# Output projection of a hybrid decoder layer: three fp32r products of split halves in place of one fp32 product, the second half of the projection token tile by token tile, and counters raised at another place

## The chip, the cores and the metric

One core of one Trainium2 chip runs the whole program. The metric is the device time of one execution in microseconds (us). Engines are named as the profile names them: PE is TensorE (PEld its weight loads), DVE VectorE, ACT ScalarE, POOL GpSimd, SP SyncE, which here only issues transfers; a q behind a name is that engine's sequencer.

## The reference, cut to what matters

```python
n = rms_norm(h, norm_mix_w)                     # h: 16 meta tokens + 512 tokens, width 1024
proj = n @ w_in                                 # conv_B | conv_C | conv_x | z | x,B,C of the SSD | dt
y_conv = grouped_rms_norm(c_b * causal_dwconv(c_c * c_x), 8 groups)
y_ssd  = grouped_rms_norm((ssd_chunked(...) + D * xs) * silu(z), 4 groups)
h = h + concat([y_conv, y_ssd]) @ w_out         # (512 x 2048) @ (2048 x 1024): the output projection
logits = rms_norm(h) @ router_w + router_b      # 32 experts, the best 4 of each token
h = h + sum of the 4 experts' clamped SwiGLU, gated
out = rms_norm(h)[16:]
```

All of it is float32. The 512 tokens give 2048 assignments to 32 experts, in blocks of up to 96 tokens per expert.

## The kernel before

Each engine has its own program in the order of the source, and they meet by semaphores: `wait_ge` stops an engine until a counter has reached a value, `then_inc` raises one when an instruction is done. An engine never passes a waiting instruction.

**Input projection and SSD.** A product of normed input and weights is made of fp32r parts. ACT copies a tile of 128x1024 weights to its rounded high part `w_hi` (L662), DVE subtracts that from the tile and gets the low part `w_lo` (L874, in the helper `split`), the input has `n_hi` and `n_lo` in the same way, and `mm3` (L1344) adds hi x hi, lo x hi and hi x lo into one PSUM bank. `w_hi` and `w_lo` have two buffers each. After 16 tiles of x, B and C come four chunks of 128 tokens (`chunk_step` on DVE, `turn_chunk` and `rest_of_chunk` on PE), which also make the conv heads and norm them (`head_norms`: two reciprocals at L964, two multiplies at L968). PE's products of a chunk (L1472) need from DVE the masked score (L996, fed by L984 to L989) and the C rows scaled by exp(a) (`e4`, L1004).

**The z tiles.** Eight tiles of 128x512 follow (k = 0 to 7, `pair(k, 0, SEQ)`, two pairs of banks in turn). ACT takes each by `Silu` (L767), DVE multiplies it onto y_ssd (L1100) and makes the low part of the weights two tiles on; `group_squares` and `group_norm` norm the four SSD groups on the way. Ahead of them DVE runs the last `head_norms` and four small router operations (L1083 to L1089).

**Output projection.** The 2048 rows of w_out are eight pieces r of 256 rows (1 MB each), the 512 tokens four tiles m. `out_proj(r, m)` (L1526, matmuls at L1530) is four fp32 matmuls of 128x128 by 128x512 that read y and w_out as they are; the profile has two records for each fp32 matmul and one for each fp32r matmul. The order is r = 0 to 3 for m = 0 to 2, then r = 4 to 7 for each of these m, and the last tile in eight steps (`last_tile`), for which w_out's pieces 0 and 1 are loaded again.

**Routing.** For each finished tile DVE adds the residual (`residual`, L1114), ACT squares it, DVE scales it and SP writes the normed rows to DRAM (`n2_scratch`, L419); PE transposes the tile (L1552), multiplies it by the router weights (`logit_parts`, `logits`), DVE chooses four experts (`choose`), PE ranks the tokens (`rank`), DVE places them (`place`, L1167 to L1177), and POOL scatters four columns of slots (L552). `pick_first` (L1595) gathers the first expert's tokens by a matmul; this part stands in small pieces between the steps of the last tile and behind it.

**Experts.** A block is `gate_up`, eight pieces q = 0 to 7 of 1 MB, and `down`, pieces 8 to 11, all at L1660. The weights lie in 12 slots of 1 MB: slots 0 to 5 in `ring`, 6 to 11 in `ring2`, which is free of the input's halves once the z tiles are through. The second expert's first two pieces go to `extra` (the regions reg_b and reg_x). SP refills a slot when PE has used it. The second expert's tokens come by POOL: four reads of the slot list (`list_rows`, L565), an add (L569), three indirect gathers (L573), then DVE turns them (L1256). `gate_up(0)` needs `x0T` (L1210), its pieces, and one count each of `xT_ready` and `gu_free`, which DVE raises by hand:

```python
            dve.sem_inc(gu_free, 1)
            dve.sem_inc(act_ready, 1)
            dve.wait_ge(bias_in, 16)
            up_bias = bias.rearrange("p (n k b) -> p n k b", k=2, b=FF_BLOCKS)[:, :, 1, :]
            v.tensor_scalar(up_bias, up_bias, 1.0, None, ALU.add).then_inc(bias_ready, 1)
            dve.sem_inc(xT_ready, 1)
```

## Time and profile before

| | us |
|---|---|
| median of 3 runs (1581.72 to 1583.81) | 1582.28 |
| the profiled execution, whole | 1586.74 |
| its span in the trace | 1585.1 |
| PE / DVE / ACT / POOL busy in the span | 1531.7 / 584.9 / 228.5 / 330.5 |

The span is one execution from its first to its last instruction, and all places below are microseconds from its start. A busy engine is in an instruction's record, and PE's records overlap, so that the pitch from start to start says what a matmul costs. A chain row is a piece of the chain of work that ended last; a number in square brackets behind a timeline row is the idle time ahead of it with what released it.

### The profile page before, as it was taken

The page shows a single profiled execution, that of the slowest core. Times are in us where ns is not written, and L with a number is a line of the kernel's source. Part 1 is how long each engine was busy: PE and PEld are TensorE (multiplying, and loading weights), DVE is VectorE, ACT ScalarE, POOL GpSimd, SP SyncE. Part 2 cuts the span into 40 slices and gives each one's busy share as a digit, 9 for nine tenths or more (in the row PEclk, how much of TensorE's full clock was granted, in tenths as well). Part 3 has the DMA queues.
Part 4 walks back from the last instruction along what each step waited for, and adds up shares of the span by engine and source line. Part 5 has one row for each costly group of instructions (what it writes and reads, how often), then busy time and mean ns, then how long its engine had stood idle before and what let it go on. Part 6 is the DMA issues. An engine that isn't in the chain of part 4 may idle for free.

```text
span 1585.1 us, 37739 instructions
## 1 busy us (share of the span) xinstructions
PE 1531.7 (97%) x15275; PEld 1000.5 (63%) x15275; DVE 584.9 (37%) x1221; ACT 228.5 (14%) x316; POOL 330.5 (21%) x512
## 2 busy tenths in 40 slices
PE   9999999999996999999999999999999999999996
PEld 7998899774442455655654665666556566666562
DVE  6777988862134321122211321122211321122225
ACT  4533443240021000000000000000000000000001
POOL 1000000000024232223322232223322232223320
PEclk9999999999998999999999999999999999999998
DMA  4232222334254999999999999999999999999936
GB/s 148 81 125 86 88 77 104 159 143 166 89 192 160 380 399 406 403 410 405 398 407 401 407 403 398 408 407 404 400 405 407 408 404 399 407 413 404 396 121 271
DMA packets 80788, 479.09 MB, mean 302 GB/s; under 512 B 17410, under 2 KB 18058, under 8 KB 26610
## 3 DMA queue, kind: packets, MB, share of 16 engines
q1 hardware_dynamic: 66354, 461.24, 73.0%
q0 software_dynamic: 14400, 17.37, 3.1%
q8 instruction: 24, 0.39, 0.1%
q14 instruction: 10, 0.08, 0.0%
HBM read 470.03 MB, written 17.01 MB: 307 GB/s over the span
## 4 chain that ended last, share of the span: by engine, by line
PE 92%; DVE 5%; issue 1%; DMA 1%; ACT 1%; POOLq 0%; SPq 0%; DVEq 0%; POOL 0%; ACTq 0%
PE bank L1660 65%; PE bank L1344 15%; PE bank L1530 7%; DMA moe_f<-in_b_gate_up 1%; PE bank L1363 1%; PE bank L1472 0%; PE bank L1475 0%; DVE w_lo L874 0%; PE bank L1473 0%; PE bank L1502 0%; DVE reg_tq L964 0%; DVE reg_tq L890 0%; PE bank L1487 0%; DVE reg_vcs L869 0%; PE bank L1721 0%
## 5 line engine op out<-in xcount | busy, mean ns | idle before, releaser
L1660 PE MATMUL bank<-ring,moe_f 128*32 128x512 f32 (+1 forms) x12240 | 1023.7, 486 | 21.9 <-DVEq L1264 10.1
L1660 PEld LDWEIGHTS bank<-ring,moe_f 128*32 128x32 f32 x12240 | 620.1, 110 | 425.0 <-issue 261.5
L1275 DVE STREAM_TRANSPOSE moe_f<-bank 128x768 f32<-128x768 f32 x32 | 31.4, 983 | 617.5 <-PE bank L1660 617.5
L1344 PE MATMUL bank<-n_hi,w_hi 128*128 128x258 f32 (+2 forms) x608 | 190.8, 314 | 7.2 <-DVE w_lo L874 4.9
L573 POOL DMA_INDIRECT moe_f<-n_scratch,idx_next x99 | 103.7, 1047 | 450.8 <-DVE moe_f L1256 415.3
L1344 PE MATMUL bank<-n_lo,w_hi 128*128 128x258 f32 (+2 forms) x608 | 187.1, 308 | 0.0
L1344 PE MATMUL bank<-n_hi,w_lo 128*128 128x258 f32 (+2 forms) x608 | 187.0, 308 | 0.0
L824 ACT ACTIVATE moe_f<-moe_f 128x768 f32<-128x768 f32 x32 | 27.1, 845 | 718.1 <-DVE moe_f L1279 718.1
L1344 PEld LDWEIGHTS bank<-n_hi,w_hi 128*128 128x128 f32 x608 | 115.0, 189 | 16.2 <-DVE w_lo L874 5.4
L580 POOL DMA_INDIRECT expert_rows<-moe_f,idx_now x96 | 98.5, 1026 | 104.5 <-ACT moe_f L830 82.9
L1344 PEld LDWEIGHTS bank<-n_lo,w_hi 128*128 128x128 f32 x608 | 115.0, 189 | 6.5 <-issue 1.2
L1344 PEld LDWEIGHTS bank<-n_hi,w_lo 128*128 128x128 f32 x608 | 114.9, 189 | 5.7
L1530 PE MATMUL bank<-ring,reg_vcs 128*128 128x512 f32 x256 | 111.9, 594 | 0.0
L1293 DVE TENSOR_TENSOR moe_f<-moe_f 128x768 f32<-128x768 f32 x32 | 30.7, 959 | 160.8 <-PE bank L1660 160.7
L1530 PEld LDWEIGHTS bank<-ring,reg_vcs 128*128 128x128 f32 x256 | 48.0, 190 | 57.8 <-issue 57.8
L565 POOL DMA_DIRECT2D idx_raw<-slot_table x140 | 72.7, 529 | 8.8 <-issue 8.4
L552 POOL DMA_INDIRECT slot_table<-val,pos_i x16 | 16.6, 1035 | 223.3 <-DVE pos_i L1177 219.6
L830 ACT COPY moe_f<-bank 128x768 f32<-128x768 f32 x32 | 25.6, 801 | 247.8 <-PE bank L1660 247.8
L874 DVE TENSOR_TENSOR w_lo<-ring,w_hi 128x1024 fp32r<-128x1024 f32 x48 | 58.5, 1220 | 5.7 <-ACT w_hi L662 5.7
L662 ACT CAST w_hi<-ring 128x1024 fp32r<-128x1024 f32 x48 | 50.6, 1054 | 50.2 <-PE bank L1344 49.9
L1285 DVE TENSOR_SCALAR moe_f<-moe_f 128x96 f32<-128x96 f32 x256 | 47.6, 262 | 0.0
L1279 DVE TENSOR_SCALAR moe_f<-moe_f 128x96 f32<-128x96 f32 x256 | 47.5, 261 | 0.0
(249 smaller groups left out, 806.5 us busy)
## 6 DMA issues: line engine op xcount, KB each, us to landing
ring<-in_moe SPq DMA_DIRECT2D x382, 1024.0 KB, 7.4
ring<-in_w_in SPq DMA_DIRECT2D x24, 1024.0 KB, 4.8
ring<-in_w_out SPq DMA_DIRECT2D x10, 1024.0 KB, 4.9
ring<-expert_rows SPq DMA_DIRECT2D x8, 1024.0 KB, 12.1
ring<-acs_scratch SPq DMA_DIRECT2D x4, 1024.0 KB, 7.6
idx_raw<-slot_table POOLq DMA_DIRECT2D x140, 0.8 KB
reg_vcs<-in_xT SPq DMA_DIRECT2D x4, 528.0 KB, 6.0
reg_x<-in_xrow SPq DMA_DIRECT2D x4, 512.0 KB, 6.1
```

Source lines behind the costliest of these rows:

```text
L565: pool.dma_start(idx_raw[l * LANE:(l + 1) * LANE, :], table_d[ds(base, BLOCK), :].rearrange("(r g) t -> r (g t)", g=GRANULES)).then_inc(id ...
L573: g.indirect_dma_start(out=xg[:, n, :], out_offset=None, in_=n2_parts, in_offset=bass.IndirectOffsetOnAxis(ap=idx_next[:, 2 * n:2 * n + 1] ...
L580: g.indirect_dma_start(out=yk_parts, in_=y_sb[:, n, :], in_offset=None, out_offset=bass.IndirectOffsetOnAxis(ap=idx_now[:, 2 * n + 1:2 * n ...
L662: a.copy(w_hi[:, n % 2, :], slot(s)[:, t * KC * P:(t + 1) * KC * P]).then_inc(wh_ready, 1)
L874: v.tensor_tensor(w_lo[:, n % 2, :], slot(s)[:, t * KC * P:(t + 1) * KC * P], w_hi[:, n % 2, :].bitcast(F32), ALU.subtract).then_inc(wl_re ...
L1275: v.transpose(glu.rearrange("p b (g r) -> p g b r", g=GRANULES), gate).then_inc(gate_raw, 1)
L1279: ins = v.tensor_scalar(glu[:, b, :], glu[:, b, :], bias_col(0, b), LIMIT, ALU.add, ALU.min)
L1285: ins = v.tensor_scalar(up[:, b, :], up[:, b, :], bias_col(1, b), 1.0 - LIMIT, ALU.add, ALU.max)
L1293: v.tensor_tensor(act_t, up, sig, ALU.mult).then_inc(act_ready, 1)
L1344: ins = mm(out, w[:, n % 2, c * P:(c + 1) * P], x[:, c, first:first + width], start=c == 0 and m == 0, stop=c == KC - 1 and m == 2)
L1530: ins = mm(bank[:, 2 * m + hf, :], y[:, (2 * r + e) % KC, m * P:(m + 1) * P], slot(s)[:, e * D + hf * 512:e * D + (hf + 1) * 512], start=f ...
L1660: ins = mm(out[l * LANE:(l + 1) * LANE, g * width:(g + 1) * width], x[:, at, g * LANE:(g + 1) * LANE], w[:, l * width:(l + 1) * width], st ...
```

## The change

- `out_proj(r, m)` is twelve fp32r matmuls. ACT makes the high parts of w_out (`out_high`) and y (`y_high`), DVE the low parts (`out_low`, `y_low`). The low part of a w_out piece is written over the piece. The high parts of pieces 4 to 7 lie in slots 6 to 9, those of the second half of y in slots 10 and 11, those of the first half of y in the two extra regions.
- All four tiles run through r = 0 to 3, then each tile through r = 4 to 7, with the routing of the tile before it and `pick_first` of the one before that between its steps. w_out's pieces 0 and 1 are loaded once.
- SP loads the first expert's pieces 0 and 1 after the first half of the projection and the other ten from the last tile on.
- `xT_ready`, `gu_free` and `act_ready` are raised right behind `x0T`.
- In the first chunk `e4` comes ahead of the score; in all of them ACT's `Exp` of it comes ahead of the copy of B. The first z tile uses a bank that needs no wait, DVE makes the third z tile's low part between the last two reciprocals, and the router operations come after the group norms.

```diff
@@ kernel body: where the high and low parts lie @@
+        def out_hi(r):
+            return view(late_r, r * PIECE, PIECE) if r < 4 else view(ring2_r, (r - 4) * PIECE, PIECE)
+        def out_lo(r):
+            return view(ring_r, WOUT_SLOT[r] * PIECE, PIECE)
+        def y_hi(t):
+            if t < KC:
+                return view([reg_b_r, reg_x_r][t // 4], t % 4 * SEQ, SEQ)
+            return view(ring2_r, 4 * PIECE + (t - KC) * SEQ, SEQ)
+        def y_lo(t):
+            return view(vcs_r, (2 + t) * SEQ, SEQ)
@@ sync @@
-            sp.wait_ge(tile_done, TD_C + KC)
-            for q in range(SLOTS, PIECES):
+            sp.wait_ge(wout_used, 4)
...
+            for q in range(2):
                 sp.dma_start(slot(q), moe_d[0, q]).then_inc(w_in[q], 16)
             for m in range(TT):
+                if m == TT - 1:
+                    for n in range(4):
+                        sp.wait_ge(wout_used, 5 + n)
+                        for q in (2 + n, SLOTS + n):
+                            sp.dma_start(slot(q), moe_d[0, q]).then_inc(w_in[q], 16)
+                    for q in range(SLOTS + 4, PIECES):
+                        sp.dma_start(slot(q), moe_d[0, q]).then_inc(w_in[q], 16)
+                    sp.wait_ge(h2_ready, TT)
+                    sp.dma_start(extra[1][:, :], moe_d[1, 1]).then_inc(extra_in[1], 16)
                 sp.wait_ge(n2_ready, m + 1)
                 sp.dma_start(n2_d[m * P:(m + 1) * P, :], n2b[:, m % 2, :]).then_inc(n2_out[m % 2], 16)
...
@@ scalar @@
+            def out_high(r):
+                act.wait_ge(w_in[WOUT_SLOT[r]], 16 * WOUT_USE[r])
...
+                a.copy(out_hi(r), slot(WOUT_SLOT[r])).then_inc(out_hi_ready, 1)
...
+                if k == 4:
+                    out_high(0)
+                    y_high(0)
+                    y_high(1)
+                if k == 6:
+                    out_high(1)
...
@@ vector @@
-            head_norms(TT)
+            head_norms(TT, between=lambda: split_z(2))
...
+            def out_low(r):
+                dve.wait_ge(out_hi_ready, r + 1)
+                w = slot(WOUT_SLOT[r])
+                v.tensor_tensor(out_lo(r), w, out_hi(r).bitcast(F32), ALU.subtract).then_inc(out_lo_ready, 1)
...
+                if k == 5:
+                    out_low(0)
+                    y_low(0)
+                    y_low(1)
+            out_low(1)
...
+            for m in range(TT - 1):
+                residual(m)
+                root_mean(m)
+                scaled(m)
+                choose(m)
+                gated(m)
+                place(m)
             residual(3)
-            place(2)
...
+            dve.sem_inc(xT_ready, 1)
+            dve.sem_inc(gu_free, 1)
+            dve.sem_inc(act_ready, 1)
             gated(3)
@@ tensor @@
+            def out_proj(r, m):
+                pe.wait_ge(out_lo_ready, r + 1)
+                pe.wait_ge(y_lo_ready, 2 * r + 2)
                 for e in range(2):
+                    t = 2 * r + e
+                    yh, yl = y_hi(t)[:, m * P:(m + 1) * P], y_lo(t)[:, m * P:(m + 1) * P]
                     for hf in range(2):
+                        cols = slice(e * D + hf * 512, e * D + (hf + 1) * 512)
+                        for n, (y, w) in enumerate(((yh, out_hi(r)), (yh, out_lo(r)), (yl, out_hi(r)))):
+                            ins = mm(bank[:, 2 * m + hf, :], y, w[:, cols], start=t == 0 and n == 0,
+                                     stop=t == 2 * KC - 1 and n == 2)
...
+            pe.wait_ge(rs_raw, GROUPS)
+            for r in range(2):
+                out_proj(r, 3).then_inc(wout_used, 1)
+            for r in range(2, 4):
+                for m in range(TT):
+                    ins = out_proj(r, m)
+                ins.then_inc(wout_used, 1)
...
+            for r in range(4, 8):
+                ins = out_proj(r, 0)
+            ins.then_inc(out_done, 1)
+            for m in range(1, TT):
                 for r in range(4, 8):
+                    ins = out_proj(r, m)
...
+                    if r == 4:
+                        if m > 1:
+                            rank(m - 2)
+                        n2_transposes(m - 1)
+                    if r == 5:
+                        logit_parts(m - 1)
+                        if m > 1:
+                            pick_first(m - 2, 0)
+                    if r == 6:
+                        logits(m - 1)
+                        if m > 1:
+                            pick_first(m - 2, 1)
+            rank(2)
+            n2_transposes(3)
```

How instructions move on DVE ahead of the z tiles (reg_tq holds the roots of the norms, reg_vcs y and silu(z), w_lo the low parts). Before:

```order
L964 RECIPROCAL reg_tq<-reg_tq 128x512 [waits rs_root]
L964 RECIPROCAL reg_tq<-reg_tq 128x512
L968 SCALAR_TENSOR_TENSOR reg_vcs<-reg_vcs,par,reg_tq 128x512 [waits dve_steps]
L968 SCALAR_TENSOR_TENSOR reg_vcs<-reg_vcs,par,reg_tq 128x512
L1083 TENSOR_TENSOR rw<-rw,par 128x256 [waits router_in,yc_ready]
L1086 TENSOR_TENSOR reg_a<-ident 128x32 [waits slot_iota_ready]
L1089 TENSOR_TENSOR reg_a<-reg_a,ident 128x32 [waits dve_steps] x2
L1100 TENSOR_TENSOR reg_vcs<-reg_vcs 128x512 [waits free_a,y_free]
L874 TENSOR_TENSOR w_lo<-ring,w_hi 128x1024 [waits wh_ready]
```

And in the changed kernel, whose lines have other numbers:

```order
L1022 RECIPROCAL reg_tq<-reg_tq 128x512 [waits rs_root]
L932 TENSOR_TENSOR w_lo<-ring,w_hi 128x1024 [waits wh_ready]
L1022 RECIPROCAL reg_tq<-reg_tq 128x512
L1028 SCALAR_TENSOR_TENSOR reg_vcs<-reg_vcs,par,reg_tq 128x512 [waits dve_steps]
L1028 SCALAR_TENSOR_TENSOR reg_vcs<-reg_vcs,par,reg_tq 128x512
L1168 TENSOR_TENSOR reg_vcs<-reg_vcs 128x512 [waits free_a,y_free,yc_ready]
L1168 TENSOR_TENSOR reg_vcs<-reg_vcs 128x512 [waits free_b]
L932 TENSOR_TENSOR w_lo<-ring,w_hi 128x1024 [waits wh_ready]
```

The subtraction that PE's third z tile needs now stands between the reciprocals, and the router operations are gone from here.

On DVE again, around the residual of tile 3 (reg_a<-reg_x,bank is the residual, reg_a<-bank,iota_cap the first operation of a placing). Before, the residual comes first:

```order
L1162 TENSOR_SCALAR gates<-gates,small 128x4 [waits dve_steps]
L1114 TENSOR_TENSOR reg_a<-reg_x,bank 128x1024 [waits x_res_in1,wout_used]
L1167 TENSOR_TENSOR reg_a<-bank,iota_cap 128x32 [waits rank_done]
L1169 TENSOR_SCALAR reg_a<-reg_a 128x96 [waits dve_steps]
L1171 TENSOR_TENSOR reg_a<-reg_a 128x128
```

Now the placing of tile 2 comes first, and the same order stands at the residuals of tiles 1 and 2:

```order
L1263 TENSOR_TENSOR reg_a<-bank,iota_cap 128x32 [waits rank_done]
L1265 TENSOR_SCALAR reg_a<-reg_a 128x96 [waits dve_steps]
L1267 TENSOR_TENSOR reg_a<-reg_a 128x128
L1271 TENSOR_REDUCE pos_f<-reg_a 128x4 [waits dve_steps]
L1273 CAST pos_i<-pos_f 128x4 [waits dve_steps]
L1210 TENSOR_TENSOR reg_a<-reg_x,bank 128x1024 [waits x_res_in1,wout_used]
```

A placing waits for PE's rank, which stands two tiles on, directly ahead of the transposes that need the residual.

On SP, the first expert's pieces in the last tile. Before, with six more such rows at the end of the z tiles:

```order
L419 DMA n_scratch<-reg_b 128x1024 [waits n2_ready]
L400 DMA ring<-in_w_out 128x2048 [waits wout_used] x2
L430 DMA ring<-in_moe 128x2048 [waits wout_used] x6
L419 DMA n_scratch<-reg_b 128x1024 [waits n2_ready]
L435 DMA reg_b<-in_moe 128x2048 [waits h2_ready,n2_out1,n2_out0]
```

And now:

```order
L451 DMA ring<-in_moe 128x2048 [waits wout_used]
L451 DMA ring<-in_moe 128x2048
...
L453 DMA ring<-in_moe 128x2048 x2
L456 DMA reg_x<-in_moe 128x2048 [waits h2_ready]
L458 DMA n_scratch<-reg_b 128x1024 [waits n2_ready]
L463 DMA reg_b<-in_moe 128x2048 [waits n2_out1,n2_out0]
```

The first two rows stand four times in a row; ten pieces and one of the second expert's now lie in SP's queue ahead of the last write of normed rows.

## Rows read from the trace of the kernel before

**Rows 1.** Page: the chain that ended last, by line.

```profile
PE bank L1660 65%; PE bank L1344 15%; PE bank L1530 7%; DMA moe_f<-in_b_gate_up 1%; PE bank L1363 1%; PE bank L1472 0%; PE bank L1475 0%; DVE w_lo L874 0%; PE bank L1473 0%; PE bank L1502 0%; DVE reg_tq L964 0%; DVE reg_tq L890 0%; PE bank L1487 0%; DVE reg_vcs L869 0%; PE bank L1721 0%
```

**Rows 2.** PE's own waits: line <- releaser: us in total, times, longest.

```profile
PE bank L1660 <- DVEq L1264: 10.1, 1, 10.1
...
PE bank L1344 <- DVE w_lo L874: 4.9, 3, 3.9
PE bank L1344 <- DVE reg_tq L1057: 2.2, 1, 2.2
PE bank L1472 <- DVE ring L1004: 2.1, 1, 2.1
```

**Rows 3.** Chain, 335 to 527: start, us, what.

```profile
335.09 11.12 PE bank L1344 x48
...
372.78 58.37 PE bank L1530 x136
...
478.21 1.23 DVE reg_a L1114
...
502.25 22.23 PE bank L1660 x192
...
526.49 28.67 PE bank L1660 x336
```

**Rows 4.** PE's timeline: start, us, engine, line, operation.

```profile
484.23 2.79 PE L1595 MATMUL bank<-reg_a 128*96 128x512 f32 x6
```

**Rows 5.** Stretches: us, busy PE, PEld, DVE, ACT, POOL; clock, DMA share, GB/s.

```profile
317.00:360.00 43.00, 39.59 (x155) 30.37 (x156) 24.29 (x27) 19.17 (x25) 0.00 (x0) 0.96 0.39 147
320.80:324.30 3.50, 3.50 (x10) 2.72 (x9) 1.52 (x2) 1.04 (x2) 0.00 (x0) 0.51 0.79 276
388.00:400.00 12.00, 12.00 (x29) 5.32 (x28) 0.00 (x0) 0.00 (x0) 0.00 (x0) 1.00 1.01 427
502.25:526.49 24.24, 22.77 (x197) 7.02 (x198) 3.08 (x6) 1.21 (x2) 8.67 (x17) 0.94 0.61 208
558.80:1540.00 981.20, 969.69 (x11639) 596.33 (x11634) 226.86 (x639) 50.18 (x61) 274.12 (x423) 1.00 0.98 395
```

**Rows 6.** DVE's and ACT's timelines, one row of each kind.

```profile
467.59 0.19 DVE L1167 TENSOR_TENSOR reg_a<-bank,iota_cap 128x32 f32<-128x32 f32 x1 [2.29 <-PE bank L1581]
...
468.71 0.17 DVE L1177 CAST pos_i<-pos_f 128x4 uint32<-128x4 f32 x1
...
142.34 2.28 DVE L996 TENSOR_TENSOR ring<-ring,reg_b 128x2048 f32<-128x2048 f32 x1
...
318.54 0.69 DVE L1100 TENSOR_TENSOR reg_vcs<-reg_vcs 128x512 f32<-128x512 f32 x1
...
131.61 1.92 ACT L730 ACTIVATE ring<-ring 128x2048 f32<-128x2048 f32 x1 [0.46 <-DVE ring L942]
```

**Rows 7.** Behind the projection: DVE's, then POOL's timeline.

```profile
488.94 0.17 DVE L1177 CAST pos_i<-pos_f 128x4 uint32<-128x4 f32 x1
...
491.82 1.02 DVE L1210 TENSOR_TENSOR moe_f<-bank,par 128x384 f32<-128x384 f32 x2 [0.71 <-PE bank L1650]
...
514.20 0.98 DVE L1256 STREAM_TRANSPOSE moe_f<-moe_f 128x768 f32<-128x768 f32 x1 [11.80 <-DMA moe_f<-n_scratch,idx_next]
...
500.88 2.24 POOL L565 DMA_DIRECT2D idx_raw<-slot_table  x4 [5.90 <-issue]
...
510.57 1.00 POOL L573 DMA_INDIRECT moe_f<-n_scratch,idx_next  x1 [0.30 <-issue]
...
538.41 0.19 POOL L569 TENSOR_TENSOR idx_next<-idx_raw,lane_off 128x6 int32<-128x6 int32 x1 [4.37 <-DMA moe_f<-n_scratch,idx_next]
```

**Rows 8.** DMA issues: tiles, count, KB each, us to landing.

```profile
n_scratch<-reg_b SPq DMA_DIRECT2D x4, 512.0 KB, 2.7
...
block_list<-more_i SPq DMA_DIRECT2D x1, 0.2 KB, 7.0
```

**Rows 9.** The tile `ring` from 1350 to 1480: us from issue to landing.

```profile
DMA to landing us min/median/max: 7.1/7.7/8.5
```

More of the change, by code:

```diff
@@ L124, in build @@
         with nc.sbuf_tensor("reg_vcs", [P, (2 + 2 * KC) * SEQ], F32) as reg_vcs:
+            pass
+        with nc.sbuf_tensor("vcs_r", [P, (2 + 2 * KC) * SEQ], F32R) as vcs_r:
             pass
@@ L408, in _ @@
             sp.dma_start(reg_k[:, :], rows_d).then_inc(rows_in, 16)
-            for m in range(2):
-                sp.dma_start(x_res[:, m, :], xrow_d[m * P:(m + 1) * P, :]).then_inc(x_res_in[m], 16)
             for r in (6, 7):
@@ L766, in _ @@
                     act.wait_ge(yz_ready, k - 1)
-                a.activation(z_sb[:, k % 2, :], pair(k, 0, SEQ), ACT.Silu).then_inc(free[k % 2], 1)
+                a.activation(z_sb[:, k % 2, :], pair(k, int(k == 0), SEQ), ACT.Silu).then_inc(free[k % 2], 1)
                 if k + 2 < KC:
@@ L964, in head_norms @@
                     steps.done(v.reciprocal(sqb[:, t, 0:SEQ], sqb[:, t, 0:SEQ]))
+                    if t == 0 and between is not None:
+                        between()
                 steps.settled()
@@ L981, in halved, with scaled_c @@
                     return halves_b(i, n)
+                def scaled_c():
+                    dve.wait_ge(e_ready, i + 1)
+                    steps.done(v.tensor_copy(dec[:, :], acs_b[:, :, P - 1]))
+                    e4 = acs_b.rearrange("p (g r) l -> p g r l", g=GROUPS)
+                    dve.wait_ge(chunk_ready, i + 1)
+                    steps.settled()
+                    v.tensor_tensor(e4, e4, chunk[:, 12:16, :].unsqueeze(2).to_broadcast([P, GROUPS, PER_GROUP, P]), ALU.mult
+                                    ).then_inc(cs_ready, 1)
+                if not third:
+                    scaled_c()
                 dve.wait_ge(tok_done, i * 3 + 2 + 3)
@@ L997, in chunk_step @@
                                 ).then_inc(score_ready, 1)
[L999 to L1005 removed]
+                if third:
+                    scaled_c()
                 def short_conv(k, t):
@@ L1177, in place @@
                 v.tensor_copy(pos_i[:, m * TOPK:(m + 1) * TOPK], pm).then_inc(pos_ready, 1)
-            residual(0)
-            root_mean(0)
-            scaled(0)
-            residual(1)
-            root_mean(1)
-            scaled(1)
-            choose(0)
-            gated(0)
-            residual(2)
-            root_mean(2)
-            place(0)
-            scaled(2)
-            choose(1)
-            gated(1)
-            place(1)
-            choose(2)
-            gated(2)
+            for m in range(TT - 1):
+                residual(m)
[4 more added lines that the diff above has]
+                place(m)
             residual(3)
-            place(2)
             root_mean(3)
```

198 lines of the change are left out of this document (94 added, 104 removed).

## The prediction

> **What bounds the kernel now.** I read the chain by line first [rows 1]: 65% of the span is PE in the expert blocks, 15% the input projection's fp32r products, 7% the output projection's fp32 ones. The reader is to see that PE is the bound nearly everywhere, so that time goes only with PE's work or with one of its waits. PE's waits come next [rows 2]. The largest is 10.1 us: the first expert's first product waits for a counter of DVE. Its tokens `x0T` are ready at 492.84 (row of L1210), but the counter comes behind DVE's wait for the biases' transfer, and PE starts at 502.25 [rows 3, 7]. Three smaller ones are 3.9 us for the third z tile's low part, 2.2 us for the first z tile's bank, and 2.1 us for `e4` in the first chunk. The chain in order of time [rows 3] gives three marks: the projection runs to T = 478.2, where DVE's last residual starts; `gate_up(0)` starts at T + 24.0; `gate_up(1)` at 526.5, T + 48.3. From there the blocks are one even stretch to 1540 with the clock at its upper level [rows 5], and I take it that they move as a whole with the start of `gate_up(1)`. So the forecast is that start.
>
> **Ahead of the projection.** In the first chunk `e4` takes the place where DVE waits for PE's masked products; the score is then done about when PE is through with its tile: -2.0 of the 2.1. The first z tile needs no bank: -2.2. The third z tile's low part moves ahead of 3.3 us of reciprocal and some 2.3 us of multiplies and router work, so the 3.9 us wait goes, and with it what followed that wait: for 3.5 us from 320.8 the granted clock was 0.51, that is the 1.2 GHz level [rows 5], and half of that stretch, 1.7 us, was lost. What is late next is the fourth tile's low part: DVE must finish the norms and two multiplies before it. I take 1.0 us for this new wait (none if DVE is just in time, 2.5 if it is behind by one more multiply and ACT's copy). Sum: -2.0 - 2.2 - 3.9 - 1.7 + 1.0 = **-8.8**.
>
> **The projection's matmuls.** Before, 8 pieces x 4 tiles x 4 = 128 fp32 matmuls; 136 records, two each, took 58.37 us, so one is 0.858 us and all are 109.9. Now there are 384 fp32r matmuls. The nearest rows have the same shape and the same kind of operands: 48 in 11.12 us, each with a weight load of its own, so one is 0.232 and all are 89.0 [rows 3]. **-20.9**.
>
> **Making the halves.** Each piece costs ACT one copy of 128x2048 (the activation of that size is 1.92) and two of 128x512 (some 0.6), DVE a subtraction of 2.28 and two of 0.69 [rows 6]: 3.1 and 3.7 us, for all eight 25 and 29 us. PE uses a piece for 11.1 us (48 x 0.232) in the first half. In the z tiles DVE waits again and again for PE (busy 24.3 of 43 us there, rows 5), and the first piece's halves, after the sixth z tile's multiply, are ready some 8 us before PE asks. Group norms of 3.4 us of reciprocal lie between, and PE's new wait for the last group's `rs_raw` comes 18 us into the projection: DVE is through with it a little earlier. Pieces 4 to 7 are asked for from 46 us on; w_out's last two transfers are issued 21 and 24 us in, and copy, subtraction and landing (7.7 us) end by 38. I cost all this at nothing; its cover is the z tiles' slack and the first half's 44 us. Without it: 0 to 4 us.
>
> **The second half.** `pick_first` of tiles 0 and 1, four matmuls, moves from the gaps behind T to before it: three took 2.79 [rows 4], so +3.7, nothing given back behind T, where the chain runs over DVE and ACT. Then the new order on DVE: PE issues `rank`, directly behind it transposes that need the next residual, and DVE does the placing (467.59 to 468.88, 1.3 us, rows 6) and then the residual (1.22, rows 3) while PE stands with nothing else ahead of it. That is 2.6 us with signals, twice before T (tiles 2 and 3): +5.2. Before, the residual was made while PE was in other work. The end of the projection is then T' = 478.2 - 8.8 - 20.9 + 3.7 + 5.2 = **457.4**.
>
> **From T' to `gate_up(0)`.** The same wait stands at the last tile: 2.6 instead of the 1.3 from T to the transposes, +1.3. `x0T` came at T + 14.6; it comes at T' + 15.9, and since the counters stand right behind it, `gate_up(0)` starts at 473.3 instead of 502.25. From its start to that of `gate_up(1)` 24.2 us passed at a mean clock of 0.94 [rows 5], since it began at the lower level after 10 us of idle PE: 6% of it, 1.4 us, goes with the idle time. PE is ready for `gate_up(1)` at 473.3 + 22.8 = 496.1.
>
> **The second expert's tokens.** This chain was hidden and is now as long as PE's. The fourth tile's places were written at 489.1, T + 10.9; POOL read its list from 500.88, 11.8 us later, and DVE had turned the tokens at 515.2, another 14.3 [rows 7]. Now: 457.4 + 10.9 + 1.3 + 11.8 = 481.4, turned at 495.7, just before PE is ready. POOL also waits for the last normed rows to be in DRAM, and these lie behind eleven 1 MB transfers in SP's queue. The transfers may start at the third `scaled`, about T' - 7.5. At 427 GB/s [rows 5] one is 2.5 us; two us to the first byte and 27.5 for eleven gives T' + 22, the rows land at about T' + 23.7 = 481.1. That they wait is seen in the trace: 0.2 KB behind some 2.5 MB landed in 7.0 us, 512 KB in an empty queue in 2.7 [rows 8]. The Trainium skill ("DMA: Bandwidth & Descriptors", section "Queues, rings and completion order") says that each DMA engine consumes a queue's descriptors in ring order, and the trace agrees; if small transfers overtook large ones, the rows would be down at T' + 16 and the sum would be the same, since the places' own 11.8 us end later. Both branches thus end at 481, and I add 1.0 us for the company of SP's transfers: `gate_up(1)` at **497.1**, 29.4 before the 526.5. The first expert's pieces are no limit: piece 5, the last that `gate_up(0)` needs, is the seventh in SP's order and down at about T' + 12, before PE even starts.
>
> **Sum.** -8.8 - 20.9 + 3.7 + 5.2 = -20.8 at T'; then +1.3 (the order), -9.5 (the counter, 24.05 - 14.6), -1.4 (clock), +1.0: -29.4. The sum is against the profiled execution, 1586.74 with its span of 1585.1. The median, 1582.28, is 0.3% lower; nothing in the terms depends on that, so 1582.3 - 29.4 = **1552.9 us**. A change of 0.2% is what a measurement of this kernel can tell.
>
> **Rivals.**
> *The tokens come late.* While SP's transfers fill the engines, POOL's own are slower: POOL waited 4.37 us more for the gather that fell into busy transfers (538.41), and the one before it, in a quiet stretch, was down 2.6 us after its last issue (511.57 to 514.20, rows 7). The chain has three such legs, the scatter, the list and the gather, 2 us each: +6 less the 1 I took, 1558. In this case most of what raising the counters gains is lost again: the change does its edit but not its saving. The skill's same section says that an engine takes turns between the queues that have work, packet by packet; by that POOL's small transfers pay at each leg but never wait for SP's whole queue, which is this rival's size. For it: DMA is busy until T' + 24 and again with the extras. Against: the scatter's and list's 11.8 and 14.3 us hold waits that are no DMA time.
> *The halves come late.* DVE or ACT falls behind at piece 0, at `rs_raw` or at pieces 6 and 7; each is 2 to 4 us of PE standing, and up to 1.7 of clock behind one as after the 3.9 us wait: +8, 1561. For it: both are strict sequences with group norms inside. Against: 29 us of work under 89.
> *The transfers bound the expert blocks.* DMA is busy 0.98 of the time there at 395 GB/s [rows 5]. Were it the bound, only the start of the stream would count, which comes forward with T': -20.8, 1561.5. Against: a piece lands 7.7 us after issue even late in the run, 8.5 at most [rows 9], and is needed some 25 us after that.
> *Slower: PE runs the projection at the lower level.* If PE waits for halves at piece after piece, the clock stays down, as the 0.51 of rows 5 shows for one wait, and a matmul costs up to twice 0.232: 384 x 0.464 = 178 us, +89 on the forecast, 1642. It decides from a mean pitch of 0.232 + 29.4 / 384 = 0.309 us. Against: PE has 11 us of work per piece and DVE needs 3.7.
>
> **How the numbers follow.** Forecast 0.60, tokens late 0.15, halves late 0.13, transfers bound 0.06, slower 0.02; no change, several of these together, 0.04. The forecast's own range is 1549 to 1557 (the fourth z tile 0 to 2.5, contention 0 to 3, one stretch at the lower clock 0 to 1.7, and 3 us the other way if new waits overlap). With the next three cases the range for 8 in 10 is **1547 to 1564**. Faster by over 0.2%: 0.96; within: 0.02; slower: 0.02.
>
> **What would show it.** Right: no wait of PE at z tile 1 or 3 and less than 2.5 at tile 4; 384 records at a pitch of 0.232; two waits of about 2.6 us of the transposes for the residual, a third behind the projection; its end near 457; `gate_up(0)` near 473, `gate_up(1)` near 497 and waiting, if at all, for DVE's L1256 rows; the last write of normed rows landing some 10 us after issue instead of 2.7; expert blocks 32.4 us apart as before. Wrong: waits at the projection's matmuls for `out_lo` or `y_lo`, a clock below 1 in them, PE waiting for a piece in `gate_up`, or blocks further apart.

## The result and the profile after

The changed kernel takes **1566.6 us** (median of 4 runs, 1565.2 to 1569.8) where the kernel before took 1583.1 beside it: ratio 0.9896, 95% interval 0.9875 to 0.9918. It is faster, as forecast, but by 16.5 us and not by 29.4. The forecast was 1552.9, and the time is 2.6 us above its range. Beside the kernel before on two other chips, further below, the same kernel gained 20.1 and 20.5 us. One of its executions there took 2574 us at a mean granted clock of 0.56, and no median or ratio here counts it. The profiled execution took 1567.67 with a span of 1566.0.

`gate_up(2)` starts 16.1 us ahead of the kernel before (542.5 against 558.6), which is the gain of the medians to 0.4 us, so nearly everything is decided before that start. The two spans differ by 19.1, because from there to their last product the blocks took 982.6 us in this profile and 985.9 in that of before: the same untouched blocks take 982.5 to 983.7 us on two of the chips used below and 985.8 to 986.8 on two others. Only medians and ratios of kernels run side by side are free of this. PE's waits between 350 and 545, the rows that answer to [rows 2]:

```profile
PE bank L1732 <- issue: 8.3, 1, 8.3
PE bank L1641 <- DVE reg_a L1210: 7.5, 3, 2.5
PE bank L1667 <- DVE reg_a L1241: 1.8, 1, 1.8
PE bank L1621 <- issue: 1.5, 1, 1.5
```

The 10.1 us for the counter are gone. Their place is taken by 8.3 us of the same line, now ahead of the second expert's `gate_up` instead of the first's. Next the chain in order of time, which answers to [rows 3]:

```profile
353.09 8.41 PE bank L1621 x36
...
363.22 48.97 PE bank L1621 x216
...
460.03 1.23 DVE reg_a L1210
...
470.32 1.30 DVE reg_b L1224
471.63 14.12 DMA n_scratch<-reg_b
...
488.13 5.58 DMA idx_raw<-slot_table
...
497.69 6.83 DMA moe_f<-n_scratch,idx_next
504.61 0.99 DVE moe_f L1344
505.60 1.82 issue
507.42 31.56 PE bank L1732 x336
```

Up to 460.03, DVE's last residual, the gain is 18.2 us (478.21 - 460.03). `gate_up(0)` starts at 476.50 and has gained 25.75. The chain does not run over it. Behind DVE's L1224, which makes the last normed rows, it is made of three DMAs, 14.1, 5.6 and 6.8 us long, and `gate_up(1)` starts at 507.42, 19.1 us before its old 526.49. The SP queue shows why the first of the three is so long: eight pieces, two pieces, an extra piece, and only then the fourth tile's normed rows. The last two rows are six pieces of the second expert and, from L490, two of the third.

```profile
451.20 8.28 SPq L451 DMA_DIRECT2D ring<-in_moe  x8
459.52 0.91 SPq L453 DMA_DIRECT2D ring<-in_moe  x2
461.28 0.33 SPq L456 DMA_DIRECT2D reg_x<-in_moe  x1
471.63 0.33 SPq L458 DMA_DIRECT2D n_scratch<-reg_b  x1
...
493.94 5.63 SPq L479 DMA_DIRECT2D ring<-in_moe  x6
499.67 0.96 SPq L490 DMA_DIRECT2D ring<-in_moe  x2
```

POOL's timeline and then DVE's show what came of it. POOL waits 9.37 us for the rows before it reads its list. It issues the three gathers of tokens from 494.91 on, after SP has begun on those eight pieces. The last is issued by 498.7 (the end of its row) and DVE gets its data at 504.61, 5.9 us later, where it was 2.6 in the kernel before [rows 7]. DVE then turns the tokens, which takes 1 us, and only behind that clears the two banks that `gate_up(1)` needs.

```profile
486.39 2.24 POOL L592 DMA_DIRECT2D idx_raw<-slot_table  x4 [9.37 <-DMA n_scratch<-reg_b]
493.85 0.20 POOL L596 TENSOR_TENSOR idx_next<-idx_raw,lane_off 128x6 int32<-128x6 int32 x1 [5.22 <-DMA idx_raw<-slot_table]
494.91 1.12 POOL L600 DMA_INDIRECT moe_f<-n_scratch,idx_next  x1 [0.86 <-POOL idx_next L596]
...
497.69 1.00 POOL L600 DMA_INDIRECT moe_f<-n_scratch,idx_next  x1 [0.30 <-issue]
```

```profile
504.61 0.98 DVE L1344 STREAM_TRANSPOSE moe_f<-moe_f 128x768 f32<-128x768 f32 x1 [12.47 <-DMA moe_f<-n_scratch,idx_next]
505.52 0.94 DVE L1360 STREAM_TRANSPOSE moe_f<-bank 128x768 f32<-128x768 f32 x1
506.38 0.94 DVE L1361 STREAM_TRANSPOSE moe_f<-bank 128x768 f32<-128x768 f32 x1
```

The stretches (columns as in [rows 5]) show the clock: it sits at its lower level, 1.2 GHz, behind each of the longer waits, and the last of these stretches covers the first six microseconds of `gate_up(1)`.

```profile
428.00:431.40 3.40, 3.40 (x13) 2.92 (x12) 1.20 (x3) 3.16 (x5) 2.49 (x4) 0.50 0.02 1
462.10:465.50 3.40, 3.40 (x22) 1.42 (x21) 1.01 (x3) 1.01 (x4) 2.49 (x3) 0.51 1.01 424
469.00:479.20 10.20, 8.13 (x35) 3.37 (x39) 6.71 (x23) 0.58 (x1) 5.42 (x5) 0.50 1.03 391
503.10:513.30 10.20, 5.88 (x28) 1.59 (x32) 7.46 (x21) 0.84 (x1) 2.24 (x5) 0.50 1.02 418
```

### The profile page after: what moved, and what is told of

Read it like the earlier page. It is cut to its first block, busy times and chain, and to the rows that moved or that the text cites. A ratio compares the mean times of both kernels' runs of the same rounds, so it can differ in the third digit from the quotient of the medians.

```text
span 1566.0 us, 38093 instructions
## 1 busy us (share of the span) xinstructions
PE 1512.4 (97%) x15403; PEld 1031.6 (66%) x15403; DVE 610.3 (39%) x1245; ACT 253.6 (16%) x342; POOL 329.9 (21%) x512
## 4 chain that ended last, share of the span: by engine, by line
PE 90%; DVE 5%; DMA 3%; issue 1%; ACT 1%; POOL 0%; POOLq 0%; SPq 0%; DVEq 0%; ACTq 0%
PE bank L1732 64%; PE bank L1429 15%; PE bank L1621 6%; DMA n_scratch<-reg_b 1%; DVE w_lo L932 1%; PE bank L1557 0%; PE bank L1560 0%; PE bank L1572 0%; PE bank L1558 0%; PE bank L1587 0%; DMA moe_f<-n_scratch,idx_next 0%; PE bank L1684 0%; DVE reg_tq L1022 0%; DVE reg_tq L948 0%; DMA reg_vcs<-in_xT 0%
## 5 line engine op out<-in xcount | busy, mean ns | idle before, releaser
L1732 PE MATMUL bank<-ring,moe_f 128*32 128x512 f32 (+1 forms) x12240 | 1022.5, 486 | 10.3 <-DVE moe_f L1378 1.1
L1732 PEld LDWEIGHTS bank<-ring,moe_f 128*32 128x32 f32 x12240 | 627.4, 110 | 404.9 <-issue 193.6
L1621 PE MATMUL bank<-ring_r 128*128 128x512 f32 x128 | 42.6, 414 | 0.0
L613 POOL COPY idx_now<-idx_kept 128x6 int32<-128x6 int32 x31 | 5.9, 191 | 158.9 <-DMA expert_rows<-moe_f,idx_now 158.9
```

The lines of the kernel that those rows point to most:

```text
L1621: ins = mm(bank[:, 2 * m + hf, :], y, w[:, cols], start=t == 0 and n == 0, stop=t == 2 * KC - 1 and n == 2)
L1732: ins = mm(out[l * LANE:(l + 1) * LANE, g * width:(g + 1) * width], x[:, at, g * LANE:(g + 1) * LANE], w[:, l * width:(l + 1) * width], st ...
```

## The experiments

**Theory.** The second expert's tokens set the start of `gate_up(1)`, through SP's queue (the rows' write stands behind eleven pieces), through the DMA engines (the gather shares them with pieces that the early `gate_up(0)` releases), through DVE's order, and through the clock. **Rivals.** The halves and PE's waits in the projection carry the miss; the counters gave nothing; the transfers bound everything behind. In all edits "SP", "POOL" and the rest name the engine's program. Ratios are to the kernel before on the same chip, with 95% intervals. Starts vary by 1 to 2 us between profiled executions of one kernel, so both a start and a ratio are given. "Tokens at" is when DVE starts to turn them, and the gather counts as down then.

### The changed kernel itself, twice

> The changed kernel itself, unaltered, beside the others on one chip, as the measure for them. All theories: 0.9896 of the kernel before, and the starts of its expert stages as in its first trace: gate_up(0) at 476.5, gate_up(1) at 507.4, gate_up(2) at 542.5, each to 2 us.

> The changed kernel, unaltered, again beside the next two on one chip, as the measure for them: 0.987 to 0.990 of the kernel before.

Measured: 0.987 (0.9854 to 0.9887, median 1565.1) and 0.9868 (0.985 to 0.9886, 1564.5), with `gate_up(1)` at 507.0 and 505.7 and `gate_up(2)` at 540.7 in both. The three profiles agree to 2 us; 0.987 is the measure for the rest.

### Rows' write first

```diff
             sp.wait_ge(n2_ready, m + 1)
             sp.dma_start(n2_d[...], n2b[...])
+        # behind the loop, moved from ahead of m == 3:
+        pieces 10, 11 of expert 0; extra[1]
```

> Edit on the changed kernel: SP issues the write of the fourth tile's normed rows ahead of the transfers of pieces 10 and 11 and of the extra piece, instead of behind all of them. Theory (the chain of rows in DRAM, list, gather, DVE's transpose sets gate_up(1), and SP's queue holds its first link): the write, issued near 471.5, lands near 476 instead of 485.75, POOL reads its list near 479 instead of 486.4 (then the last scatter of places, issued to 476.3, is the limit), DVE's x turned starts near 498 instead of 504.6 and gate_up(1) near 501 instead of 507.4; time down by 5 to 7 us against the changed kernel, 1560 to 1562. Rival (the transfers bound what follows, or the gather only meets other traffic): the list comes earlier but the blocks do not, time within 1 us of 1566.6. Rival (halves or clock are all of the miss): nothing before 476 moves, and gate_up(1) moves by under 1 us.

Measured: 0.9853 (0.9837 to 0.987), 2 to 3 us below the changed kernel where 5 to 7 were expected, with intervals that overlap. The write, issued at 472.65, is down at 476.5. The list moves from 486.4 to 483.7:

```profile
483.70 2.23 POOL L591 DMA_DIRECT2D idx_raw<-slot_table  x4 [5.66 <-issue]
```

Tokens at 501.65, `gate_up(1)` at 504.5, 1.3 to 3.0 us before the unaltered kernel's. So the queue is real, but only half as expensive as it looks: once the rows are down, the list waits for the last scatter of places. That was issued by 477.3, and the list follows it by 6.4 us, as it does by 5.9 in the kernel before (issued by 495, list at 500.9); POOL's program waits for both.

### The gather alone, once and again

```diff
+            sp.wait_ge(x_in, 16 * GRANULES)
             gate_up(1, 1, 2)
```

> Edit on the changed kernel: SP waits until the gather of the second expert's tokens has landed before it issues that expert's next eight pieces. Theory (the gather is slow because it shares the DMA engines with SP's 8 MB): issue of the last gather to its landing falls from some 6 us to some 2.6 as before the change, x turned near 501.3 instead of 504.6, gate_up(1) near 504 instead of 507.4; the pieces, issued 6 us later, are still there in time; 3 us faster than the changed kernel, 1563.5. Rival (what slows the gather is not company but the gather itself, or the pieces are then missing): landing still 6 us after issue and no gain, or PE waits for pieces inside gate_up(1) and the time is up by 1 to 5 us.

> The gather without SP's company, a second time, now beside the unaltered changed kernel. Its profile had gate_up(2) 7 to 9 us earlier than the changed kernel's, its median beside the kernel before only 0.986. Theory (the profile is typical, and that chip's kernel before was the odd one): 0.004 to 0.0055 below the ratio of the unaltered kernel (6 to 9 us), gate_up(1) near 501.5 and its first piece 2.6 us. Rival (the profiled execution was a lucky one, others still lose the clock): 0.001 to 0.002 below.

Measured: 0.986 (0.9843 to 0.9876), then 0.9853 (0.9838 to 0.9868) beside the control's 0.9868; medians 1562.4 against 1564.5. In both profiles the gather is down 1.8 us after its last issue, below even the 2.6 of the kernel before, where one piece went out 0.6 us behind the last issue. The second profile, POOL and DVE:

```profile
495.77 1.00 POOL L601 DMA_INDIRECT moe_f<-n_scratch,idx_next  x1 [0.30 <-issue]
```

```profile
498.58 0.98 DVE L1345 STREAM_TRANSPOSE moe_f<-moe_f 128x768 f32<-128x768 f32 x1 [8.44 <-DMA moe_f<-n_scratch,idx_next]
```

`gate_up(1)` starts at 501.35 and 501.39, 4.3 us or more ahead. What differs is the clock behind it, from 501 to 509, first execution and second:

```profile
501.00:509.00 8.00, 7.65 (x72) 2.85 (x76) 5.00 (x19) 0.85 (x1) 2.32 (x5) 1.00 1.00 414
```

```profile
501.00:509.00 8.00, 7.61 (x48) 2.25 (x52) 5.05 (x19) 0.84 (x1) 2.22 (x5) 0.63 1.01 412
```

In the same time the trace has 72 matmuls or 48. The rival of the second run was right on the size: the first profile was a lucky one. The edit brings `gate_up(1)` 4.3 us forward and is worth 2.1 by the medians, not 6 to 9. Where the rest goes is seen only in part. The first profile, which kept the clock, was the fastest of its four executions (1563.4, the others 1566.8 to 1567.0); that the others lost the clock is likely, not shown. The second profile and the control's beside it pay the same for their first two pieces (5.1 and 2.8 us), and of the 4.6 us at `gate_up(2)` (536.1 against 540.7) 1.1 are lost in the blocks behind it (983.5 us against 982.5) and 1.2 behind the blocks; why was not looked into.

### Rows' write first and gather alone

Both edits above; nothing on DVE or PE is changed.

> Two edits on the changed kernel, none of which touches DVE or PE: SP issues the rows' write ahead of its last three pieces and of the gather's rivals (e1 and e2 together). Theory (the forecast's chain was right but for SP's queue): list near 483.5, gather down 1.8 us after its issue near 497, tokens turned by 498; PE is through with gate_up(0) at 498.5 and clears the banks; gate_up(1) at 500.5: 0.0055 to 0.0065 below the unaltered kernel (9 to 10 us), a little more than the gather edit alone. Rival (the two edits free the same wait twice and nothing adds, or the late pieces now hold PE): within 0.001 of the gather edit alone, or PE waits for a piece.

Measured: **0.9826** (0.9812 to 0.9839), 1557.8 against the control's 1564.5: 6.7 us where 9 to 10 were expected, the interval clear of the control's. List at 480.6, tokens at 494.75, `gate_up(1)` at 497.6, its first piece costing 4.3 us instead of 2.6. The edits add. This start is the forecast's 497.1, although the last residual came no earlier than in the control beside it (458.2 against 458.1), and the time is 27.2 us below the kernel before, where the forecast had 29.4.

### Residual ahead of placing

```diff
             for m in range(TT - 1):
                 residual(m)
+                if m:
+                    place(m - 1)
                 root_mean(m) ... gated(m)
-                place(m)
             residual(3)
+            place(2)
```

> Edit on the changed kernel: on DVE the residual of tile m + 1 stands ahead of the placing of tile m. Theory (PE stands three times for placing and residual one behind the other): PE's three waits of 2.5 us for the residual (7.5 in all) fall to 0 to 1.3 each; the end of the projection comes 3 to 5 us earlier (454 to 456) and the part behind it is 1.3 shorter; the last places come no earlier than now relative to the end. Time down by 3 to 5 us, 1562 to 1563.5. Rival (the tokens' chain hangs on SP's queue, whose 16 transfers start at fixed releases, not on the projection's end): the projection ends earlier, but gate_up(1) comes forward by under 1.5 us, and the time with it.

Measured: 0.9837 (0.9821 to 0.9854). PE's three waits of 2.5 us are one of 1.2, DVE's last residual starts at 452.0, 8 us earlier. Some of that is clock: its mean from 353 to 458 is 1.00 instead of 0.98. But the rows, issued at 462.6, wait 16.5 us in SP's queue until 479.1, and the chain behind the projection takes it back:

```profile
PE bank L1734 <- DVE moe_f L1363: 13.3, 1, 13.3
```

`gate_up(1)` at 501.1: of 8 us, 5 to 6 arrive, and by the ratio 5. The residual's term of the forecast was real, and the queue eats part of its undoing.

### Banks ahead of the tokens

```diff
                 v.transpose(... gate).then_inc(gate_raw, 1)
                 v.transpose(... lin).then_inc(gu_free, 1)
+                if not follows:
+                    x_transposed(2)
...
-            x_transposed(2)
             activations(0, 0, False)
```

> Edit on the changed kernel: on DVE the two transposes that clear gate_up(0)'s banks stand ahead of the transpose of the second expert's tokens, instead of behind it. Theory (PE had finished gate_up(0) near 497 and then stood for the tokens and for the banks, the banks 1.8 us after the tokens): the banks are cleared near 499, gate_up(1) starts right behind the tokens' transpose, 505.6 instead of 507.4, and the time is down by 1.8 us; the activations of expert 0 come earlier too, which frees nothing else. Rival (PE waits in gate_up(1) for something else, such as its pieces): gate_up(1) starts earlier and its first products take as much longer; no change of time.

Measured: 0.9867 (0.985 to 0.9883). The mechanism shows (banks at 496.8 and 497.7, tokens at 500.92, `gate_up(1)` at 501.95, 1.0 us behind instead of 2.8), but by the ratio it is not told from the control's 0.987. The early start of this profile is no measure: it is that of the fastest of four executions (1565.2 to 1569.6).

### Counters raised late again

```diff
-            dve.sem_inc(xT_ready, 1); dve.sem_inc(gu_free, 1); dve.sem_inc(act_ready, 1)
             gated(3)
...
+            (the same, where they stood before the change, xT_ready behind the wait for bias_in)
```

> Edit on the changed kernel: the three counters are raised where they were before the change, behind DVE's wait for the biases' transfer. Theory (the tokens' chain sets gate_up(1), but only while gate_up(0) ends before it): the biases land near 491.9 in the changed kernel, so gate_up(0) starts there instead of at 476.5, ends 21 to 23 us later near 514, and gate_up(1) starts near 515.5 instead of 507.4: 8 us slower than the changed kernel, some 1574, only half of the counters' 15.4 us being of use. PE idles 33 us behind the projection instead of 18, then 1 us instead of 10. Rival (the counters give nothing since the tokens decide): within 1 us of the changed kernel.

Measured: 0.9922 (0.9907 to 0.9937), 1572.9 against 1565.1 on the same chip: 7.7 us slower.

```profile
490.64 23.40 PE L1732 MATMUL bank<-ring,moe_f 128*32 128x512 f32 x192 [16.59 <-DVEq L1349]
...
516.05 2.78 PE L1732 MATMUL bank<-reg_b,moe_f 128*32 128x512 f32 x24 [1.47 <-issue]
```

And, not expected: with `gate_up(0)` late, no piece of the second expert is in flight when the gather is (SP issues the first at 501.3), and the tokens are there at 498.86, 4 to 6 us earlier than in the changed kernel, 1.8 us after the last issue. The early counters slow the very transfer that then decides.

### The counters alone, on the kernel before

```diff
                                 ).then_inc(xT_half, 1)
+            dve.sem_inc(xT_ready, 1)
+            dve.sem_inc(gu_free, 1)
+            dve.sem_inc(act_ready, 1)
             gated(3)
...
-            (the same three, where they stood before the change)
```

> Edit on the kernel before: the three counters alone are raised right behind x0T, the rest as before. Theory (in the kernel before no write of rows waits in SP's queue, and its gather had the DMA engines to itself): gate_up(0) starts near 493 instead of 502.25 and ends near 514; the second expert's tokens are turned at 514.2 to 515.2 as before, then DVE clears two banks until 517; gate_up(1) near 517 instead of 526.5, 9.5 us faster than before, 0.994. So the term of the counters (-9.5) was right by itself and it is their company that failed. Rival (the term was wrong by itself, since gate_up(1) hangs on another wait): under 3 us of gain.

Measured: 0.9973 (0.9963 to 0.9983): 4.2 us, under half of the term. `gate_up(0)` started early enough, at 495.0, but SP's pieces for expert 1 went out from 506.3 and the gather fell among them; SP, DVE and PE:

```profile
506.29 9.97 SPq L451 DMA_DIRECT2D ring<-in_moe  x6
```

```profile
518.75 0.98 DVE L1259 STREAM_TRANSPOSE moe_f<-moe_f 128x768 f32<-128x768 f32 x1 [14.39 <-DMA moe_f<-n_scratch,idx_next]
```

```profile
521.56 4.70 PE L1660 MATMUL bank<-reg_b,moe_f 128*32 128x512 f32 x24 [5.21 <-issue]
```

### The same, with the gather alone

```diff
+            sp.wait_ge(x_in, 16 * GRANULES)
             gate_up(1, 1, 2)
```

> Edit on the kernel before: the three counters raised early, as in the run that raised them alone, and SP waits until the second expert's gather has landed before it issues that expert's eight pieces. Theory (raising the counters releases the first expert's slots earlier, so that SP's 8 MB run into the gather, which then lands 5.6 us after its last issue instead of 1.8, and PE, idle for it, comes back at the lower clock): the gather lands within 2 us, the tokens are turned before PE is through with gate_up(0), gate_up(1) starts 3 us earlier than in that run and its first piece costs 2.6 instead of 4.5: 5 us less than the 0.9973 of it, 0.994, which is the full 9.5 us of the term. Rival (the gather was late by itself, or the pieces now are): within 1.5 us of 0.9973, or PE waits for pieces.

Measured: **0.9926** (0.9912 to 0.9939), 11.5 us below the kernel before, where counter and clock together stood in the forecast at 10.9.

```profile
515.51 3.01 SPq L451 DMA_DIRECT2D ring<-in_moe  x6
```

```profile
515.51 0.98 DVE L1260 STREAM_TRANSPOSE moe_f<-moe_f 128x768 f32<-128x768 f32 x1 [11.03 <-DMA moe_f<-n_scratch,idx_next]
```

```profile
518.32 2.78 PE L1661 MATMUL bank<-reg_b,moe_f 128*32 128x512 f32 x24 [1.63 <-issue]
```

One wait on SP is the difference, each run measured beside the kernel before on its own chip, and the intervals do not meet. This pair shows, on a kernel with none of the change's other parts, that raising the counters triggers transfers, that these collide with the gather, and that the collision with the clock it costs takes more than half of the gain: 7.3 us by the medians, of which the two profiles show 3.2 in the start of `gate_up(1)` and 1.9 in its first piece. The second profile is that of the slowest of its five executions, 2.2 us above their median.

### The third z tile's low part late again

```diff
-            head_norms(TT, between=lambda: split_z(2))
+            head_norms(TT)
...
-                if 0 < k < KC - 2:
+                if k + 2 < KC:
```

> Edit on the changed kernel: the third z tile's low part is made where it was before the change, behind the norms and the first multiply. Theory (the prediction's term): PE waits again for it, 2.5 to 3.9 us, the clock falls behind that wait for 3.5 us (1.7 lost), and the fourth tile's new wait of 0.8 goes: the projection starts at 356.5 to 358 instead of 353.1, and everything behind it moves as much: 3.4 to 4.8 us slower than the changed kernel, ratio about 0.990 where that is 0.987. Rival (the z tiles' slack takes it up, as the projection waits 1.5 us for its halves anyway): under 2 us slower.

Measured: 0.9901 (0.9886 to 0.9916), against 0.987 and 0.9868 for the control on two other chips: about 5 us, with intervals that just touch. PE waits 3.0 us again and goes on at the lower clock:

```profile
314.90 0.50 PE L1429 MATMUL bank<-n_hi,w_hi 128*128 128x512 f32 x1 [3.03 <-DVE w_lo L932]
...
316.23 0.63 PE L1429 MATMUL bank<-n_lo,w_hi 128*128 128x512 f32 x1
```

The projection starts at 356.75 instead of 352.7 to 353.1. The z term was right, and the z tiles' slack takes nothing of it up.

### Four edits together, and three

Rows' write first, gather alone, residual first and banks first; then the same without banks first.

> Four edits on the changed kernel together: rows' write ahead of the last pieces (e1), gather without SP's company (e2), residual ahead of placing (e3), banks ahead of the tokens (e4). Theory: projection's end near 452 (e3's), rows' write down near 467, list near 474 to 476 (the rows of e3 waited until 479.6 with the write behind the queue), gather down 1.8 us after its issue as in e2, tokens turned near 489; gate_up(0) from 466.4 without a pause to 487, gate_up(1) near 490.5 instead of 507.4, gate_up(2) near 522.5 instead of 542.5: 20 us faster than the changed kernel, some 1547 where that is 1567. Rival (each edit frees the same wait, so that the gains of e1 to e4, 4 to 9 us by gate_up(2)'s start, do not add): about the best of them, 1558 to 1560.

> The run of four edits less one: rows' write first, gather alone, residual first, but DVE turns the tokens ahead of clearing the two banks, as in the changed kernel. Theory: with the gather alone the tokens are down at 487.6, before PE ends gate_up(0) at 489; DVE then has them turned before the banks are asked for, and gate_up(1) starts at 491.4 instead of 492.3: 0.9 us faster than 1551.5, 1550.6 (0.978). That edit helps only while the tokens come last. Rival: no difference that can be measured, or 1 us slower.

Measured: four edits 0.9785 (0.9771 to 0.9799, median 1551.5); without banks first 0.9776 (0.9763 to 0.9789). `gate_up(1)` starts at 492.3 and 491.1. In the second the tokens are down before PE is through with `gate_up(0)`, and DVE is free to turn them first:

```profile
487.65 0.98 DVE L1346 STREAM_TRANSPOSE moe_f<-moe_f 128x768 f32<-128x768 f32 x1 [4.30 <-DMA moe_f<-n_scratch,idx_next]
489.14 0.98 DVE L1362 STREAM_TRANSPOSE moe_f<-bank 128x768 f32<-128x768 f32 x1 [0.51 <-PE bank L1734]
```

The two cannot be told apart by their ratios; the order of the profiles is as expected. Either beats both kernels: four edits are 13.7 us below the changed one on the same chip, where 20 were expected, and the two are 33.7 and 36.1 us below the one before. What bounds it now is PE again, with 1.5 us of wait ahead of `gate_up(1)`:

```profile
491.09 2.78 PE L1734 MATMUL bank<-reg_b,moe_f 128*32 128x512 f32 x24 [1.48 <-issue]
```

## Why the prediction was wrong

**Ahead of the projection (-8.8): right.** The first product starts at 353.09 where it was at 360.6: -7.5 with the halves' 1.5 us in it, -9.0 without. The two runs on the kernel before, which leave this part as it was, have that start at 362.7 and 363.0, so that the one profile all these differences are taken against may be some 2 us early. The fourth z tile's new wait was 0.8 (1.0 forecast). Making the third's low part late again cost about 5 us.

**The matmuls (-20.9): right, a little small.** The pitch is 48.97 / 216 = 0.227, not 0.232, so 384 take 87.1: -22.8.

**Making the halves (nothing): off by 1.5.** PE stands 1.48 us ahead of its first product, never afterwards. It waits for no half: those of the first piece were done by 343.3. It waits for the bank of the last z tile, which ACT empties only behind its copy for the second piece's high part (L790); ACT and PE:

```profile
350.61 1.88 ACT L790 CAST late_r<-ring 128x2048 fp32r<-128x2048 f32 x1
352.40 0.59 ACT L810 ACTIVATE reg_vcs<-bank 128x512 f32<-128x512 f32 x1
```

```profile
353.09 0.47 PE L1621 MATMUL bank<-late_r,reg_b_r 128*128 128x512 f32 x1 [1.48 <-issue]
```

So making the halves held up other work of ACT, and the rival "halves late" (+8) is out but for this 1.5.

**The second half (+3.7, +5.2): right.** Three waits of 2.5 where I had 2.6. What I left out is the clock behind the first of them, 3.4 us at 0.50, some 1.7 lost. The last residual starts at 460.0 where T' + 1.3 made it 458.7.

**From T' to `gate_up(0)`: the size was off.** The order's +1.3 and the counter's place held, but of the -1.4 for the clock nothing came. PE's small products run at 0.51 from 462.1 to 465.5 and at 0.50 from 469.0 to 479.2, into `gate_up(0)`, whose first piece again costs 3.9 us. It started at 476.5, 3.2 late, 1.3 of it from T'. This did not count, since it was not last.

**The second expert's tokens: the step that failed.** It said: "Both branches thus end at 481, and I add 1.0 us for the company of SP's transfers: `gate_up(1)` at 497.1". The chain and the order of its DMAs were right; its prices were not, and DVE's link lacked the two banks. The 10.3 us that are missing at `gate_up(1)`, and 2.9 behind it, by the rows of the first profile of the changed kernel:

- the list, 486.4 instead of 481.4: +5.0. Of this 1.3 is the later T'; the rest is the rows' write, down at 485.75 and not at 481.1: from the first issue (451.20) to the landing of the eleventh (461.28 + 23.2) 33.3 us passed, and I had 29.5. The branch "small transfers overtake" is out: the write took 14.1 us where [rows 8] show 2.7, and moved ahead of the queue's last three transfers it was down 3.9 us after issue.
- from list to turned tokens 19.2 instead of 14.3 + 1.0: +3.9. List and gather each have SP's transfers beside them. The 14.3 came from a quiet stretch, and I priced company at 1.0 where the row of 538.41 already showed 4.4 for one gather.
- from turned tokens to `gate_up(1)`, 1.8 instead of 0.4: +1.4. I took PE as the last to be ready and so never asked what DVE had queued behind the tokens: the two banks.
- the clock: PE, idle for 8.3 us, pays 5.1 and 3.0 for its first two pieces instead of 2.6 each: +2.9 (two other profiles of this kernel: 1.6 and 2.8).

The sum is 13.2; the medians' gain is 12.9 short. Of the gains of 20.1 and 20.5 us measured later the miss is only 9.3 and 8.9, so the shares above hold for one pair of profiles and not to the microsecond. The rival "tokens come late" named this mechanism and had 0.15, but priced it at three legs of 2 us. It lacked the queue's excess, DVE's order and the clock. The root lies one step further back, in the term of the counter: raising it was costed as time gained for PE alone, although it also releases the slots of expert 0, and so brings eight 1 MB transfers forward into the gather. By the two runs on the kernel before, the term is worth 4.2 us in their company and 11.5 without. With the write and the gather out of that company the changed kernel starts `gate_up(1)` at 497.6.

**The transfers bound the blocks: out.** From `gate_up(2)` on the blocks run as before: on one chip 982.7 us in the changed kernel and 982.9 in the kernel before with its counters early.

**What stays open.** Why the same idle time costs the clock in one execution and not in another. The shares of queue, gather and order do not separate cleanly, since a share is worth something only while its link is last: by medians beside the unaltered kernel the gather alone gives 2.1 us, queue and gather together 6.7, all four edits 13.7; for the queue alone there is only its start of `gate_up(1)`, some 2 us earlier. Why up to 2 us of an earlier `gate_up(2)` do not reach the end was not looked into. Slowing the scatter alone was not tried.

## What to carry to other kernels

When a step is made earlier, follow what it releases, not only who waits for it: here it let 8 MB go beside the gather that decided next. One wait on the issuing queue raised the gain of the counters alone from 4.2 to 11.5 us; in the changed kernel it gave 2.1 by itself and 6.7 together with the earlier write. A small write that another engine waits for is to be issued ahead of a prefetch that nobody needs yet. And a chain that becomes the last one has to be priced anew in its new company, with the queue of every engine on it, down to two transposes behind the one that counts, and with the clock that an idle PE comes back at.

## What the runs showed of the hardware

- A gather of three indirect DMAs was down 1.8 us after its last issue where SP sent nothing beside it (six profiles), and 5.5 to 6.3 us after it with 1 MB transfers beside it (eight profiles); DVE's start tells when.
- A 512 KB write took 14.1 us behind 11 transfers of 1 MB of which part was under way (12.8 to 14.5 in seven other profiles), and 16.5 when it was issued 9 us earlier behind the same eleven. Behind eight of them it took 3.9, 6.0, 8.3 and 9.9 us (rows' write first; with the gather alone; four edits; three edits), and was down 26 to 29 us after the first of the eight was issued. So it lands when the queue ahead is through.
- The granted clock behind a wait of PE isn't the same each time: after 3.1 us idle ahead of `gate_up(1)` it stayed at 1.00 in one execution, after 4.9 us in another of the same edit it was 0.63 over the next 8 us. And idle times of 2.36 and 2.35 us in two kernels (four edits; rows and gather) were followed by a first piece of 2.6 us in one and of 4.3 in the other. After a wait of 3.0 us in the z tiles a matmul of 0.39 us took 0.63, after one of 0.8 it did not.
